# Stick-breaking attention in a two-block kernel: GpSimd sums the softplus of later key blocks, and one projection tile is cut in two between the two heads' products

## The chip, the cores and the metric

The kernel runs on one core of a Trainium2 chip. The metric is device time in microseconds of one execution, from the first to the last instruction of the program. Five engines work at the same time and wait for each other through semaphores: PE (TensorE, matrix products into the PSUM banks), DVE (VectorE, elementwise), ACT (ScalarE, activations and copies), POOL (GpSimd, elementwise, on-chip memory alone) and SP (SyncE, which issues the weight loads). All instructions of an engine run in the order in which the program lists them. A wait of one instruction therefore holds everything behind it on that engine.

## The reference, cut to what matters

The program is a whole network of two blocks. The change is in the second block's stick-breaking attention (8 heads of 64, 512 positions, key blocks of 128):

```
z = jnp.einsum('bqhd,bkhd->bhqk', qb, kb).astype(jnp.float32) * scale
causal = kpos < qpos
log_beta = jax.nn.log_sigmoid(z)
log_1mb = jnp.where(causal, jax.nn.log_sigmoid(-z), 0.0)
later = lax.cumsum(log_1mb, axis=3, reverse=True) - log_1mb
w = jnp.where(causal, jnp.exp(log_beta + later), 0.0)
outs.append(jnp.einsum('bhqk,bkhd->bqhd', w.astype(v.dtype), vb))
```

A weight thus needs the sum of softplus(z) = -log_sigmoid(-z) over all later keys up to the query. Beside this attention the second block projects its input with w_in (26 tiles of 128 columns), and those products are independent of the attention's elementwise work.

## The kernel before, in words

All products are made in a reduced 32-bit format: each operand is split into a high half (a rounded copy, made by ACT) and a low half (the rest, made by DVE as original minus high), and a product is three matmuls: high by high, high by low, low by high. The weights come in slabs of two tiles; `split(n)` on ACT makes the high half of slab n, `split(n)` on DVE the low half (one instruction of 128x2048, 2.3 us), after which `lo_done` counts up and PE may use the slab.

Scores are kept transposed: key block j on the partitions, queries j*128 to 511 along the row. So row j of `softplus` has 128 columns for j = 3 and 512 for j = 0; columns to the left of j*128 in a row are unused. The heads go in four pairs (`first` and `second`), each with its own set of buffers (`softplus` and `softplus_b`). For a pair the order is:

- PE `logits(pair)`: the scores of both heads, j from 3 to 0. The last block (j = 0) waits for the previous pair's output to be read out of its bank (`so_scaled`).
- PE then has two projection tiles, `W_BEFORE[pair]`, as cover. Meanwhile DVE takes the absolute value (`size`), ACT the exponential and logarithm, and DVE adds the positive part and masks the diagonal block with `before` (`softplus_sum`: per row one instruction with an input in PSUM, then one of 128x128 with two inputs in on-chip memory, `sp_ready`). ACT makes `sp_hi`, DVE `sp_lo`, four rows per head each.
- PE `sticks(h)`, for each j: a mask product with `not_before`; the negated sums of the later key blocks, by products with `minus` (all entries -1), high and low for each later block i; and the own block with `from_here`, high and low. ACT `weights(h)` then exponentiates.
- PE makes the projection tile `W_AFTER[pair]` after both heads' sticks, and then `stick_values(pair)`, the products with the values.

DVE's own order in a pair sets much of this: `softplus_sum` of both heads, copy of the first cover tile out of its bank (`w_out_of`), `softplus_low(first)`, copy of the second cover tile, `softplus_low(second)`, and only then `split` of a slab (n+8 in pair 0, n+10 in pair 1, n+11 in pair 2, and a further one, n+9 and n+12, in pairs 0 and 2). Tile 16, made at the end of pair 0, is of slab n+8; tile 19 (pair 1) of slab n+9; tile 22 (pair 2) of slab n+11; tile 25 (pair 3) of slab n+12, where n is the first slab of w_in.

GpSimd makes the masks earlier, and then only issues two small copies of `wk_T` by DMA.

Of the kernel before, what the change touches and what calls it, by code (L numbers as in the profile page):

```python
# [164 lines left out]
def build(nc, ins, out):  # L165
# [9 lines left out]
    with ctx:  # L175
# [209 lines left out]
        v1_stored = sem("v1_stored")  # L385
        v1_loaded = sem("v1_loaded")
# [15 lines left out]
        mixg_ready = sem("mixg_ready")  # L402
        mixg_done = sem("mixg_done")
# [11 lines left out]
        fsum_ready = sem("fsum_ready")  # L415
        stat2_done = sem("stat2_done")
        f_step = sem("f_step")
        v_ready = sem("v_ready")
        y_ready = sem("y_ready")
        col_sqrt = sem("col_sqrt")  # L420
        col_ready = sem("col_ready")
# [8 lines left out]
        pwhi_done = sem("pwhi_done")  # L430
        pwlo_done = sem("pwlo_done")
# [10 lines left out]
        ln_sqrt = sem("ln_sqrt")  # L442
# [56 lines left out]
        sp_low = sem("sp_low")  # L499
        c_ready = sem("c_ready")  # L500
# [65 lines left out]
        def stick_out(h):  # L566
            r0 = (h % 2) * HD
            return bank[3 * (h % 2)][r0:r0 + HD, :]

# [215 lines left out]
        def _(sp):  # L785
# [32 lines left out]
            for n in LOADS:  # L818
# [10 lines left out]
                if n == FIRST["pc_out"] + 2:  # L829
                    sp.wait_ge(kv_free, 32)  # L830
                    sp.dma_start(v1_dram, v1[:, :, :]).then_inc(v1_stored, 16)
                if n == FIRST["mla_o"] + 2:
                    sp.wait_ge(v1_stored, 16)
                    sp.wait_ge(lo_ready, MH // 2)
                    sp.wait_ge(q_ready, MH)
                    sp.dma_start(vN[:, :, :], v1_dram).then_inc(v1_loaded, 16)
# [13 lines left out]
        def _(pool):  # L850
# [70 lines left out]
            pool.wait_ge(tile_free, TILE0["w_in"] + 2 * W_SLABS.index(10) + 1)  # L921
            pool.dma_start(wk_T[HD:, 0, :], wk_T[0:HD, 0, :]).then_inc(k_shift, 16)
            pool.dma_start(wk_T[0:HD, 1, :], wk_T[HD:, 1, :]).then_inc(k_shift, 16)

        @block.tensor
        def _(pe):
# [76 lines left out]
            nc.tensor.transpose(bank[0][:, 0:16], prow[0:16, 0, :], ident[0:16, 0:16]).then_inc(mixg_ready, 1)  # L1003
# [112 lines left out]
            pe.wait_ge(pwlo_done, 1)  # L1116
# [336 lines left out]
            def w_tile(i):  # L1453
# [5 lines left out]
                if i == WV_TILE + 2:  # L1459
# [15 lines left out]
                else:  # L1475
                    slab_tile("w_in", n, i, o[:, :], DT,
                              lambda k: (wh[:, k, j * P:(j + 1) * P], wl[:, k, j * P:(j + 1) * P]), h_operand,
                              free=False)
# [55 lines left out]
            for pair in range(SBH // 2):  # L1534
# [101 lines left out]
            for t in range(NB):  # L1636
# [7 lines left out]
                if t == 0:  # L1644
                    pe.wait_ge(fsum_ready, 1)
# [3 lines left out]
                if t == 2:  # L1649
                    pe.wait_ge(col_sqrt, 1)  # L1650

        @block.scalar
        def _(act):
# [110 lines left out]
            act.wait_ge(mixg_done, 1)  # L1764
# [9 lines left out]
            for s in range(6):  # L1774
# [27 lines left out]
                if s == 3:  # L1802
                    act.wait_ge(small_loaded, 96)
                    a(pw_hi[:, :, :], pw_raw[:, :, :], ACT.Copy).then_inc(pwhi_done, 1)
# [22 lines left out]
            for s in range(8):  # L1827
# [17 lines left out]
                if s == 5:  # L1845
                    act.wait_ge(ln_summed, 2)
                    a(rstd[:, :], stat[:, :], ACT.Sqrt, scale=1.0 / (4 * P), bias=eps[:, :]).then_inc(ln_sqrt, 1)
# [11 lines left out]
            def cross(layer):  # L1859

                for s in range(4):
# [3 lines left out]
                    if s == 1:  # L1865
                        if layer:
                            act.wait_ge(v1_loaded, 16)
# [39 lines left out]
                if layer == 0:  # L1907
                    act.wait_ge(v1_stored, 16)
# [127 lines left out]
            act.wait_ge(v_ready, 1)  # L2036
# [37 lines left out]
            for pair in range(SBH // 2):  # L2074
# [64 lines left out]
            a(kv_col[:, :], bank[7][:, 0:NB], ACT.Sqrt, scale=1.0 / D, bias=eps[:, :]).then_inc(col_sqrt, 1)  # L2139
            act.wait_ge(col_ready, 1)  # L2140
# [6 lines left out]
        def _(dve):  # L2147
# [89 lines left out]
            dve.wait_ge(mixg_ready, 1)  # L2237
            cp(prm[:, 0, 0:16], bank[0][:, 0:16]).then_inc(mixg_done, 1)
# [40 lines left out]
            for s in range(6):  # L2279
# [16 lines left out]
                if s == 5:  # L2296
                    dve.wait_ge(pwhi_done, 1)
                    low(pw_lo[:, :, :], pw_raw[:, :, :], pw_hi[:, :, :]).then_inc(pwlo_done, 1)
# [63 lines left out]
            dve.wait_ge(ln_sqrt, 1)  # L2362
# [378 lines left out]
            stt(v_col, f_weighted, 1.0 / D, t_col, MUL, ADD).then_inc(v_ready, 1)  # L2741
            dve.wait_ge(f_step, 1)
# [13 lines left out]
            dve.wait_ge(f_step, 2)  # L2756
# [167 lines left out]
            def last_square(i):  # L2924
                dve.wait_ge(square_made, DT * len(XNORMS) + i + 1)
                if i > 1:
                    dve.wait_ge(square_added, (DT - 2) * len(XNORMS) + i - 1)
                tt(sq[0][:, :], sq[0][:, :], last_sq[i % 2][:, :], ADD)\
                    .then_inc(square_added if i < DT - 1 else fsum_ready, 1)
# [6 lines left out]
            dve.wait_ge(col_sqrt, 1)  # L2936
            nc.vector.reciprocal(kv_col[:, :], kv_col[:, :]).then_inc(col_ready, 1)
            dve.wait_ge(col_ready, 1)
# [33 lines left out]
```

## Time and profile before

| | us |
|---|---|
| runs shown | 1710.36, 1710.79, 1717.02 |
| median | 1710.79 |
| span of the profiled execution | 1710.9 |
| PE busy in it | 1684.1 |
| DVE busy | 1064.3 |
| ACT busy | 706.7 |
| POOL busy | 23.8 |

The profiled execution's span is within 0.1 us of the median of the runs, so times read from its trace can be added to the median as they are. In the trace every instruction has a start, a duration and, in brackets, the idle time of its engine before it with what ended that time. Durations of matmuls overlap, so what a matmul costs PE is read as the distance between starts. PEclk is the granted clock: 1.00 is the upper level (2.4 GHz), 0.50 the lower (1.2 GHz). The pairs run from 1510 to 1622 us.

### The profile page before, as it was taken

The page shows a single profiled execution, that of the slowest core. Times are in us where ns is not written, and L with a number is a line of the kernel's source. Part 1 is how long each engine was busy: PE and PEld are TensorE (multiplying, and loading weights), DVE is VectorE, ACT ScalarE, POOL GpSimd, SP SyncE. Part 2 cuts the span into 40 slices and gives each one's busy share as a digit, 9 for nine tenths or more (in the row PEclk, how much of TensorE's full clock was granted, in tenths as well). Part 3 has the DMA queues.
Part 4 walks back from the last instruction along what each step waited for, and adds up shares of the span by engine and source line. Part 5 has one row for each costly group of instructions (what it writes and reads, how often), then busy time and mean ns, then how long its engine had stood idle before and what let it go on. Part 6 is the DMA issues. An engine that isn't in the chain of part 4 may idle for free.

```text
span 1710.9 us, 21153 instructions
## 1 busy us (share of the span) xinstructions
PE 1684.1 (98%) x8045; PEld 1374.0 (80%) x8045; DVE 1064.3 (62%) x1513; ACT 706.7 (41%) x1138; POOL 23.8 (1%) x42
## 2 busy tenths in 40 slices
PE   8999999999999999999999999999999999999998
PEld 7888888788888888887668878888888888977776
DVE  5799763475555532478875446555555767357695
ACT  7313543443333322345764264333332113166674
POOL 1000000000000000011100000000000000000000
PEclk9999999999999999999999999999999999999999
DMA  6272522132222232311104203222227641320201
GB/s 208 82 233 79 170 83 68 50 98 90 91 92 95 98 111 93 91 62 42 50 1 148 99 25 98 98 92 92 92 94 243 202 144 57 116 80 25 75 26 49
DMA packets 154295, 164.40 MB, mean 96 GB/s; under 512 B 2999, under 2 KB 150384, under 8 KB 153968
## 3 DMA queue, kind: packets, MB, share of 16 engines
q1 hardware_dynamic: 153408, 162.51, 29.3%
q8 instruction: 48, 0.79, 0.2%
q0 software_dynamic: 336, 0.53, 0.2%
q10 hardware_dynamic: 479, 0.39, 0.1%
q14 instruction: 24, 0.19, 0.0%
HBM read 160.01 MB, written 3.15 MB: 95 GB/s over the span
## 4 chain that ended last, share of the span: by engine, by line
PE 89%; DVE 6%; ACT 3%; issue 1%; DMA 1%; SPq 0%; DVEq 0%; ACTq 0%
PE bank L928 88%; ACT xa_p L1655 1%; DVE w_lo L2159 1%; PE bank L1354 1%; DMA x_nat<-in_x_dram 1%; DVE nmax L2668 0%; DVE h_lo L2159 0%; ACT w_hi L1655 0%; DVE mla_pT_b L2680 0%; ACT mla_p L1655 0%; DVE xa_pT_lo L2159 0%; DVE fb L2748 0%; PE bank L1614 0%; DVE h_lo L2754 0%; DVE mla_q L2629 0%
## 5 line engine op out<-in xcount | busy, mean ns | idle before, releaser
L928 PE MATMUL bank<-h_hi,w_hi 128*128 128x512 f32 x1472 | 578.9, 393 | 3.1 <-DVE w_lo L2159 1.7
L928 PE MATMUL bank<-h_hi,w_lo 128*128 128x512 f32 x1472 | 573.6, 390 | 0.0
L928 PE MATMUL bank<-h_lo,w_hi 128*128 128x512 f32 x1472 | 573.3, 389 | 0.0
L2159 DVE TENSOR_TENSOR w_lo<-w_raw,w_hi 128x2048 fp32r<-128x2048 f32 (+4 forms) x142 | 286.1, 2019 | 232.1 <-ACT w_hi L1655 231.7
L1655 ACT ACTIVATE w_hi<-w_raw 128x2048 fp32r<-128x2048 f32 (+4 forms) x142 | 239.2, 1690 | 393.6 <-PE bank L928 388.1
L928 PEld LDWEIGHTS bank<-h_hi,w_hi 128*128 128x128 f32 x1472 | 276.2, 188 | 67.8 <-issue 7.1
L928 PEld LDWEIGHTS bank<-h_hi,w_lo 128*128 128x128 f32 x1472 | 276.1, 188 | 58.2
L928 PEld LDWEIGHTS bank<-h_lo,w_hi 128*128 128x128 f32 x1472 | 276.3, 188 | 57.9 <-issue 1.2
L928 PE MATMUL bank<-g_hi,w_hi 128*128 128x512 f32 x352 | 137.6, 391 | 0.0
L928 PE MATMUL bank<-g_hi,w_lo 128*128 128x512 f32 x352 | 137.1, 389 | 0.0
L928 PE MATMUL bank<-g_lo,w_hi 128*128 128x512 f32 x352 | 137.0, 389 | 0.0
L1655 ACT ACTIVATE fb<-sq,prm 128x512 f32<-128x512 f32 x44 | 35.9, 817 | 164.9 <-DVE sq L2456 164.9
L2456 DVE TENSOR_TENSOR sq<-bank,rstd 128x512 f32<-128x512 f32 x44 | 30.3, 688 | 94.6 <-PE bank L928 94.6
L2275 DVE SCALAR_TENSOR_TENSOR cv<-glu,prm,cv 128x512 f32<-128x512 f32 x120 | 80.8, 746 | 0.0
L928 PEld LDWEIGHTS bank<-g_hi,w_lo 128*128 128x128 f32 x352 | 66.1, 188 | 13.8
L928 PEld LDWEIGHTS bank<-g_hi,w_hi 128*128 128x128 f32 x352 | 66.1, 188 | 13.6
L928 PEld LDWEIGHTS bank<-g_lo,w_hi 128*128 128x128 f32 x352 | 66.1, 188 | 13.5
L1655 ACT ACTIVATE g_hi<-fb 128x512 f32 (+1 forms) x44 | 27.8, 632 | 105.1 <-DVE fb L2471 105.1
L928 PE MATMUL bank<-m,w_whole 128*128 128x256 f32 x256 | 55.9, 379 | 0.0
L2386 DVE TENSOR_TENSOR x<-x,bank 128x512 f32<-128x512 f32 x32 | 21.9, 685 | 54.5 <-PE bank L928 54.5
L928 PEld LDWEIGHTS bank<-m,w_whole 128*128 128x128 f32 x256 | 48.7, 190 | 6.7
L928 PE MATMUL bank<-mla_k,mla_q 96*128 96x512 f32 (+3 forms) x128 | 42.8, 456 | 0.0
(374 smaller groups left out, 2052.3 us busy)
## 6 DMA issues: line engine op xcount, KB each, us to landing
w_raw<-in_ffn_w_up_dram SPq DMA_DIRECT2D x44, 1024.0 KB, 5.1
w_raw<-in_ffn_w_down_dram SPq DMA_DIRECT2D x16, 1024.0 KB, 5.1
w_raw<-in_w_in_dram SPq DMA_DIRECT2D x13, 1024.0 KB, 5.3
w_whole<-in_xa_wkv_dram SPq DMA_DIRECT2D x12, 1024.0 KB, 5.4
ada_w<-in_w_ada_dram SPq DMA_DIRECT2D x12, 1024.0 KB, 7.8
w_raw<-in_xa_wq_dram SPq DMA_DIRECT2D x8, 1024.0 KB, 5.1
w_raw<-in_xa_wo_dram SPq DMA_DIRECT2D x8, 1024.0 KB, 5.1
w_raw<-in_pc_w_in_dram SPq DMA_DIRECT2D x6, 1024.0 KB, 5.3
```

The lines of the kernel that those rows point to most:

```text
L928: return nc.tensor.matmul(o, w, v, start=start, stop=stop, **kw)
L1354: m = nc.tensor.transpose(o[:, (i - j) * P:(i - j + 1) * P], weights_of(h, i)[:, j * P:(j + 1) * P], ident[:, :])
L1655: return nc.scalar.activation(o, i, f, **kw)
L2159: return tt(lo_, v, hi.bitcast(f32), SUB)
L2275: m = stt(o, src, w, o, MUL, ADD)
L2386: tt(x[:, i, :], x[:, i, :], tile_bank(stage, i)[:, :], ADD).then_inc(tile_free, 1)
L2456: tt(sq[j][:, :], bank[(tile + j) % 4][:, :], rstd[:, :], MUL).then_inc(tile_free, 1)
```

## The change

GpSimd gets four instructions per head that write into the unused left parts of the softplus rows: row 2 gets in columns 0 to 127 a copy of its own block and in 128 to 255 the sum of rows 3 and 2; row 3 gets in columns 0 to 127 a copy of row 1's, and in 128 to 383 the sum of row 1 and row 2's left part. So for j = 1 and j = 0 one product with `minus` per half takes the place of two and three. ACT and DVE now split five pieces per head (128, 512, 384, 384 and 512 columns) instead of four (128, 256, 384 and 512). PE makes the first half (k 0 to 3) of the tile `W_AFTER[pair]` between the two heads' sticks and the second half after them. The two small DMAs of `wk_T` now stand behind the GpSimd instructions of the first two heads. Some semaphores are merged, with the same waits in effect (left out below).

```diff
+        SP_ROWS = ((3, slice(3 * P, T)), (2, slice(0, T)), (1, slice(P, T)), (3, slice(0, 3 * P)), (0, slice(0, T)))
+        SP_NEEDED = {3: 2, 2: 2, 1: 3, 0: 5}
+        BEHIND = {2: (3, slice(3 * P, T)), 1: (2, slice(0, 2 * P)), 0: (3, slice(0, 3 * P))}
...
-            pool.wait_ge(tile_free, TILE0["w_in"] + 2 * W_SLABS.index(10) + 1)
-            pool.dma_start(wk_T[HD:, 0, :], wk_T[0:HD, 0, :]).then_inc(k_shift, 16)
-            pool.dma_start(wk_T[0:HD, 1, :], wk_T[HD:, 1, :]).then_inc(k_shift, 16)
+            for h in range(SBH):
+                one, two, three = (softplus[h % 2][:, i, :] for i in (1, 2, 3))
+                pool.wait_ge(sp_ready, 4 * h + 2)
+                nc.gpsimd.tensor_copy(two[:, 0:P], two[:, 2 * P:3 * P]).then_inc(sum_step, 1)
+                nc.gpsimd.tensor_tensor(two[:, P:2 * P], two[:, 3 * P:], three[:, 3 * P:], ADD).then_inc(sum_ready, 1)
+                pool.wait_ge(sp_ready, 4 * h + 3)
+                nc.gpsimd.tensor_copy(three[:, 0:P], one[:, P:2 * P]).then_inc(sum_step, 1)
+                pool.wait_ge(sum_ready, 2 * h + 1)
+                nc.gpsimd.tensor_tensor(three[:, P:3 * P], one[:, 2 * P:], two[:, 0:2 * P], ADD).then_inc(sum_ready, 1)
+                if h == 1:
...
             def sticks(h):
 
                 for j in range(NB - 1, -1, -1):
-                    pe.wait_ge(sp_low, 4 * h + NB - min(j, 2))
+                    pe.wait_ge(sp_low, 5 * h + SP_NEEDED[j])
                     o = stick(h, j)
                     mm(o[:, 0:P], not_before[:, :], ident_b[:, :], False, False, skip_group_check=True)
-                    for i in range(NB - 1, j, -1):
+                    if j in BEHIND:
+                        i, c = BEHIND[j]
                         for part in (sp_hi, sp_lo):
-                            mm(o[:, (i - j) * P:(NB - j) * P], minus[:, :], part[h % 2][:, i, i * P:], False, False,
-                               skip_group_check=True)
+                            mm(o[:, P:(NB - j) * P], minus[:, :], part[h % 2][:, i, c], False, False, skip_group_check=True)
...
                 sticks(2 * pair)
+                w_tile(W_AFTER[pair][0], 0, DT // 2)
                 sticks(2 * pair + 1)
-                for i in W_AFTER[pair]:
-                    w_tile(i)
+                w_tile(W_AFTER[pair][0], DT // 2, DT)
                 stick_values(pair)
...
-                    for j in range(NB - 1, -1, -1):
-                        act.wait_ge(sp_ready, 4 * h + NB - j)
-                        a(sp_hi[h % 2][:, j, j * P:], softplus[h % 2][:, j, j * P:], ACT.Copy).then_inc(sp_high, 1)
+                    for n_, (i, c) in enumerate(SP_ROWS):
+                        act.wait_ge(sp_ready, 4 * h + (1, 2, 3, 3, 4)[n_])
+                        if n_ in (1, 3):
+                            act.wait_ge(sum_step, 2 * h + (n_ + 1) // 2)
+                            act.wait_ge(sum_ready, 2 * h + (n_ + 1) // 2)
+                        a(sp_hi[h % 2][:, i, c], softplus[h % 2][:, i, c], ACT.Copy).then_inc(sp_high, 1)
...
             def softplus_low(h):
-                for j in range(NB - 1, -1, -1):
-                    dve.wait_ge(sp_high, 4 * h + NB - j)
-                    v = slice(j * P, T)
-                    low(sp_lo[h % 2][:, j, v], softplus[h % 2][:, j, v], sp_hi[h % 2][:, j, v]).then_inc(sp_low, 1)
+                for n_, (i, c) in enumerate(SP_ROWS):
+                    dve.wait_ge(sp_high, 5 * h + n_ + 1)
+                    if n_ < 2:
+                        dve.wait_ge(sum_step, 2 * h + n_ + 1)
+                        dve.wait_ge(sum_ready, 2 * h + n_ + 1)
+                    low(sp_lo[h % 2][:, i, c], softplus[h % 2][:, i, c], sp_hi[h % 2][:, i, c]).then_inc(sp_low, 1)
```

On PE, in pair 0, the end of the first head's sticks before (j = 0: the mask product, three pairs with `minus`, the own block) and the start of the second head's (`_hi_156`, `_lo_154`):

```order
L928 MATMUL bank<-ident_b,not_before 128x128 [waits sp_low]
L928 MATMUL bank<-softplus_hi_155,minus 128x128
L928 MATMUL bank<-softplus_lo_153,minus 128x128
L928 MATMUL bank<-softplus_hi_155,minus 128x256
L928 MATMUL bank<-softplus_lo_153,minus 128x256
L928 MATMUL bank<-softplus_hi_155,minus 128x384
L928 MATMUL bank<-softplus_lo_153,minus 128x384
L928 MATMUL bank<-softplus_hi_155,from_here 128x512
L928 MATMUL bank<-softplus_lo_153,from_here 128x512
L928 MATMUL bank<-ident_b,not_before 128x128 [waits sp_low]
L928 MATMUL bank<-softplus_hi_156,from_here 128x128
```

The same place after the change; `w_hi_55` and `w_lo_57` are the halves of slab n+8 and the row with them the first of tile 16:

```order
L937 MATMUL bank<-ident_b,not_before 128x128 [waits sp_low]
L937 MATMUL bank<-softplus_hi_155,minus 128x384
L937 MATMUL bank<-softplus_lo_153,minus 128x384
L937 MATMUL bank<-softplus_hi_155,from_here 128x512
L937 MATMUL bank<-softplus_lo_153,from_here 128x512
L937 MATMUL bank<-h_hi,w_hi_55 128x512 [waits tile_free,lo_done]
L937 MATMUL bank<-h_lo,w_hi_55 128x512
```

Four of the products with `minus` are gone here (two more for j = 1), and tile 16, with its wait for `lo_done`, has come ahead of the second head's sticks. In pair 2 tile 22 moves in the same way.

On DVE, in pair 0, the low halves of both heads after the change, with the copies of the cover tiles (`sb_gate<-bank`) and the split of slab n+8 (the last row):

```order
L2793 COPY sb_gate<-bank 128x512 [waits slab_half]
L2173 TENSOR_TENSOR softplus_lo_153<-softplus,softplus_hi_155 128x128 [waits sum_ready,sum_step,sp_high]
L2173 TENSOR_TENSOR softplus_lo_153<-softplus,softplus_hi_155 128x512 [waits sum_ready,sum_step,sp_high]
L2173 TENSOR_TENSOR softplus_lo_153<-softplus,softplus_hi_155 128x384 [waits sp_high] x2
L2173 TENSOR_TENSOR softplus_lo_153<-softplus,softplus_hi_155 128x512 [waits sp_high]
L2793 COPY sb_gate<-bank 128x512 [waits slab_half]
L2173 TENSOR_TENSOR softplus_lo_154<-softplus_b,softplus_hi_156 128x128 [waits sum_ready,sum_step,sp_high]
L2173 TENSOR_TENSOR softplus_lo_154<-softplus_b,softplus_hi_156 128x512 [waits sum_ready,sum_step,sp_high]
L2173 TENSOR_TENSOR softplus_lo_154<-softplus_b,softplus_hi_156 128x384 [waits sp_high] x2
L2173 TENSOR_TENSOR softplus_lo_154<-softplus_b,softplus_hi_156 128x512 [waits sp_high]
L2173 TENSOR_TENSOR w_lo_57<-w_raw_53,w_hi_55 128x2048 [waits hi_done]
```

The split has kept its place behind the second head's low halves, which have one more row of 384 columns and one of 512 in place of 256.

On POOL, the first head's four instructions after the change; there were none here before:

```order
L923 COPY softplus<-softplus 128x128 [waits sp_ready]
L924 TENSOR_TENSOR softplus<-softplus 128x128
L926 COPY softplus<-softplus 128x128 [waits sp_ready]
L928 TENSOR_TENSOR softplus<-softplus 128x256 [waits sum_ready]
L923 COPY softplus_b<-softplus_b 128x128 [waits sp_ready]
```

The last row is the second head's first, which waits for that head's second masked row.

## Rows read from the trace of the kernel before

**Rows 1.** The page's busy times of the engines, with their share of the span.
```profile
PE 1684.1 (98%) x8045; PEld 1374.0 (80%) x8045; DVE 1064.3 (62%) x1513; ACT 706.7 (41%) x1138; POOL 23.8 (1%) x42
```

**Rows 2.** Windows of the four pairs, PE alone: length, busy, clock, DMA.
```profile
1512.00:1537.80 25.80, 25.80 (x140) 1.00 0.23 73
...
sum 110.10, PE 109.91; mean PE 27.48
```

**Rows 3.** The chain that ended last, up to the end of pair 0: start, us, what.
```profile
1443.15 94.62 PE bank L928 x536
```

**Rows 4.** Timeline of PE in pair 0: start, duration, instruction.
```profile
1523.35 0.23 PE L928 MATMUL bank<-ident_b,not_before 128*128 128x128 bf16 x1
...
1524.28 0.31 PE L928 MATMUL bank<-softplus_hi,minus 128*128 128x128 f32 x1
...
1524.54 0.33 PE L928 MATMUL bank<-softplus_hi,minus 128*128 128x256 f32 x1
...
1525.21 0.30 PE L928 MATMUL bank<-softplus_hi,minus 128*128 128x128 f32 x1
...
1525.76 0.34 PE L928 MATMUL bank<-softplus_hi,minus 128*128 128x384 f32 x1
...
1529.79 0.40 PE L928 MATMUL bank<-h_hi,w_hi 128*128 128x512 f32 x1
...
1535.35 0.64 PE L928 MATMUL bank<-sb_w,sb_v 128*64 128x512 f32 x1
```

**Rows 5.** Timeline of DVE in pair 0: second masked row, low halves, copy, split.
```profile
1515.59 0.29 DVE L2814 TENSOR_TENSOR softplus<-softplus,before 128x128 f32<-128x128 f32 x1
...
1521.03 1.69 DVE L2159 TENSOR_TENSOR softplus_lo<-softplus,softplus_hi 128x128 fp32r<-128x128 f32 x4
1523.54 0.69 DVE L2779 COPY sb_gate<-bank 128x512 f32<-128x512 f32 x1 [0.82 <-PE bank L928]
1524.15 1.69 DVE L2159 TENSOR_TENSOR softplus_lo<-softplus_b,softplus_hi 128x128 fp32r<-128x128 f32 x4
1525.76 2.29 DVE L2159 TENSOR_TENSOR w_lo<-w_raw,w_hi 128x2048 fp32r<-128x2048 f32 x1
```

**Rows 6.** Timelines of PE and DVE in pair 2.
```profile
1579.82 0.23 PE L928 MATMUL bank<-ident_b,not_before 128*128 128x128 bf16 x1
1580.02 0.69 DVE L2788 COPY sw_gate<-bank 128x512 f32<-128x512 f32 x1 [0.70 <-PE bank L928]
1582.23 2.29 DVE L2159 TENSOR_TENSOR w_lo<-w_raw,w_hi 128x2048 fp32r<-128x2048 f32 x1
```

**Rows 7.** Timeline of ACT in pair 0: behind the high halves; the last exponentials.
```profile
1521.63 1.90 ACT L1655 ACTIVATE w_hi<-w_raw 128x2048 fp32r<-128x2048 f32 x1
...
1531.44 1.45 ACT L1655 ACTIVATE sb_w_b<-bank 128x128 f32<-128x128 f32 x4
```

**Rows 8.** Groups of POOL instructions by shape: busy us, mean ns, idle before.
```profile
L907 POOL TENSOR_TENSOR sq<-sq,rope_sin 128x512 f32<-128x512 f32 x4 | 5.1, 1278 | 88.4 <-DVE sq L2637 88.4
...
L902 POOL TENSOR_TENSOR kpe_raw<-kpe_raw,rope_cos 32x512 f32<-32x512 f32 x1 | 1.6, 1615 | 0.1
...
L857 POOL TENSOR_SCALAR_AFFINE_SELECT ident<-ident 128x128 f32<-128x128 f32 x1 | 0.3, 292 | 0.2 <-POOL iota_i L855 0.2
```

**Rows 9.** Groups of DVE by shape, 700 to 900 us, same columns.
```profile
L2210 DVE SCALAR_TENSOR_TENSOR ckv_lo<-ckv_raw,prm,ckv_hi 128x512 fp32r<-128x512 f32 x2 | 2.9, 1484 | 0.0
...
L2210 DVE SCALAR_TENSOR_TENSOR cq_lo<-cq_raw,prm,cq_hi 128x512 fp32r<-128x512 f32 x3 | 2.1, 745 | 0.0
```

**Rows 10.** Timelines of POOL and DVE where both work.
```profile
802.54 1.37 DVE L2629 SCALAR_TENSOR_TENSOR mla_q<-bank,rstd 64x512 f32<-64x512 f32 x2
...
802.79 1.27 POOL L907 TENSOR_TENSOR sq<-sq,rope_sin 128x512 f32<-128x512 f32 x1 [16.12 <-DVE sq L2637]
```

**Rows 11.** A PE idle time, and windows' busy times and clock behind it.
```profile
806.11 0.22 PE L928 MATMUL bank<-later_b,ident_b 128*128 128x128 bf16 x1 [2.52 <-ACT fb L1655]
...
807.40:810.80 3.40, 3.40 (x13) 2.55 (x12) 3.37 (x9) 2.97 (x7) 0.00 (x0) 0.50 0.00 0
```

More of the change, by code:

```diff
@@ L499, in build @@
         sp_low = sem("sp_low")
+        sum_step = sem("sum_step")
+        sum_ready = sem("sum_ready")
         c_ready = sem("c_ready")
@@ L919, in _ @@
                                     pattern=[[1, P]], channel_multiplier=-1).then_inc(sb_masks, 1)
-            pool.wait_ge(tile_free, TILE0["w_in"] + 2 * W_SLABS.index(10) + 1)
-            pool.dma_start(wk_T[HD:, 0, :], wk_T[0:HD, 0, :]).then_inc(k_shift, 16)
-            pool.dma_start(wk_T[0:HD, 1, :], wk_T[HD:, 1, :]).then_inc(k_shift, 16)
+            for h in range(SBH):
[8 more added lines that the diff above has]
+                if h == 1:
+                    pool.wait_ge(tile_free, TILE0["w_in"] + 2 * W_SLABS.index(10) + 1)
+                    pool.dma_start(wk_T[HD:, 0, :], wk_T[0:HD, 0, :]).then_inc(k_shift, 16)
+                    pool.dma_start(wk_T[0:HD, 1, :], wk_T[HD:, 1, :]).then_inc(k_shift, 16)
         @block.tensor
@@ L1450, in _, with w_tile @@
             ada_columns(ADA // 2 - 1)
-            def w_tile(i):
+            def w_tile(i, k0=0, k1=DT):
                 s, j = i // 2, i % 2
@@ L1458, in w_tile @@
                 wh, wl = view(w_hi[pair_of(n)], DT, 256), view(w_lo[pair_of(n)], DT, 256)
-                if i == WV_TILE + 2:
+                if k0:
+                    pass
+                elif i == WV_TILE + 2:
                     pe.wait_ge(tile_free, TILE0["w_in"] + i)
@@ L1475, in w_tile @@
                 else:
-                    slab_tile("w_in", n, i, o[:, :], DT,
-                              lambda k: (wh[:, k, j * P:(j + 1) * P], wl[:, k, j * P:(j + 1) * P]), h_operand,
-                              free=False)
+                    slab_tile("w_in", n, i, o[:, :], k1 - k0,
+                              lambda k: (wh[:, k0 + k, j * P:(j + 1) * P], wl[:, k0 + k, j * P:(j + 1) * P]), h_operand,
+                              first=k0 == 0, last=k1 == DT, k0=k0, inc=1 if k1 == DT else 0, free=False)
             n = FIRST["w_in"]
@@ L1644, in _ @@
                 if t == 0:
-                    pe.wait_ge(fsum_ready, 1)
+                    pe.wait_ge(f_sums, 3)
                     for b in range(NB):
@@ L1649, in _ @@
                 if t == 2:
-                    pe.wait_ge(col_sqrt, 1)
+                    pe.wait_ge(col_step, 1)
         @block.scalar
@@ L1803, in _ @@
                     act.wait_ge(small_loaded, 96)
-                    a(pw_hi[:, :, :], pw_raw[:, :, :], ACT.Copy).then_inc(pwhi_done, 1)
+                    a(pw_hi[:, :, :], pw_raw[:, :, :], ACT.Copy).then_inc(pw_split, 1)
                 if s == 4:
@@ L1846, in _ @@
                     act.wait_ge(ln_summed, 2)
-                    a(rstd[:, :], stat[:, :], ACT.Sqrt, scale=1.0 / (4 * P), bias=eps[:, :]).then_inc(ln_sqrt, 1)
+                    a(rstd[:, :], stat[:, :], ACT.Sqrt, scale=1.0 / (4 * P), bias=eps[:, :]).then_inc(ln_summed, 1)
                 if s == 6:
@@ L2033, in _ @@
             cross(1)
-            act.wait_ge(v_ready, 1)
+            act.wait_ge(f_step, 1)
             a(r_col, v_col, ACT.Sqrt).then_inc(f_step, 1)
@@ L2138, in _ @@
             act.wait_ge(stat2_done, 4)
-            a(kv_col[:, :], bank[7][:, 0:NB], ACT.Sqrt, scale=1.0 / D, bias=eps[:, :]).then_inc(col_sqrt, 1)
-            act.wait_ge(col_ready, 1)
+            a(kv_col[:, :], bank[7][:, 0:NB], ACT.Sqrt, scale=1.0 / D, bias=eps[:, :]).then_inc(col_step, 1)
+            act.wait_ge(col_step, 2)
             for t in range(NB):
@@ L2235, in pre_copy @@
                     cp(memn[:, r - 4 - DT, :], b[:, 0:MEM]).then_inc(pre_done, 1)
-            dve.wait_ge(mixg_ready, 1)
-            cp(prm[:, 0, 0:16], bank[0][:, 0:16]).then_inc(mixg_done, 1)
+            dve.wait_ge(mixg_step, 1)
+            cp(prm[:, 0, 0:16], bank[0][:, 0:16]).then_inc(mixg_step, 1)
             dve.wait_ge(first_hi, 1)
@@ L2296, in _ @@
                 if s == 5:
-                    dve.wait_ge(pwhi_done, 1)
-                    low(pw_lo[:, :, :], pw_raw[:, :, :], pw_hi[:, :, :]).then_inc(pwlo_done, 1)
+                    dve.wait_ge(pw_split, 1)
+                    low(pw_lo[:, :, :], pw_raw[:, :, :], pw_hi[:, :, :]).then_inc(pw_split, 1)
                 for j in range(2):
@@ L2935, in _ @@
             last_square(DT - 1)
-            dve.wait_ge(col_sqrt, 1)
-            nc.vector.reciprocal(kv_col[:, :], kv_col[:, :]).then_inc(col_ready, 1)
-            dve.wait_ge(col_ready, 1)
+            dve.wait_ge(col_step, 1)
+            nc.vector.reciprocal(kv_col[:, :], kv_col[:, :]).then_inc(col_step, 1)
+            dve.wait_ge(col_step, 2)
             for t in range(NB):
```

41 lines of the change are left out of this document (17 added, 24 removed).

## The prediction

> **What bounds the kernel now.** I read the page's busy times first: PE works 98% of the span, DVE 62%, ACT 41%, POOL 1% [rows 1]. Such a share is an average, so next come windows over the four pairs of heads: PE is busy 109.91 of 110.10 us there, at the upper clock throughout [rows 2]. The chain that ended last agrees: up to the end of pair 0 it runs 94.62 us through PE without a break [rows 3]. So in this stage time is what PE has to do. A product taken from PE is worth its whole slot, and every new wait of PE costs its whole length. Last come the timelines of PE, DVE and ACT in the pairs, for how early each input of PE is ready [rows 4 to 7].
>
> **What PE is spared.** In one head the two products with `minus` for j = 1 that fall away take from 1524.28 to 1524.54, 0.26 us; the four for j = 0 take from 1525.21 to 1525.76, 0.55 us [rows 4]. That is 0.81 us per head and 6.5 us for eight. The sticks of both heads take from 1523.35 to 1529.79, so 3.22 us each; after the change 2.41 us.
>
> **What DVE and ACT get on top.** A head's low halves cover 1280 columns now and 1920 afterwards. Four instructions take 1.61 us until the next one begins (1524.15 to 1525.76) [rows 5]; in proportion 2.42 us, 0.8 us more per head. ACT's high halves grow by about as much, 1.6 us a pair. They were finished at 1521.63 [rows 7]; at 1523.2 they are still ahead of the second head's low halves, which begin at 1524.15 [rows 5]. That costs nothing; without this cover it would be those 1.6 us.
>
> **The tile that is cut in two.** This decides the sign. Tile 16 in pair 0 and tile 22 in pair 2 come from a slab whose low half DVE makes only behind the second head's low halves of that same pair, as the order of DVE shows. Before, PE asked for that slab at 1529.79 and DVE had it at 1525.76 + 2.29 = 1528.05 [rows 4, 5]: 1.7 us to spare. Now PE asks after the first head's sticks, at 1523.35 + 2.41 = 1525.76. DVE is later than before: its first 0.8 us go into the 0.82 us that it idled before copying the second cover tile, the second 0.8 us do not, and the slab is ready at 1528.85. PE waits 3.1 us. In pair 2 PE asks at 1579.82 + 2.41 = 1582.23, DVE's idle time is 0.70 us, and the slab is ready at 1582.23 + 2.29 + 0.8 + 0.1 = 1585.42: 3.2 us [rows 6]. Queued behind the waiting tile on PE are the second head's sticks, the tile's second half and the values; the whole pair shifts. Tiles 19 and 25 are of slabs that were split a pair earlier, so pairs 1 and 3 have no such wait. Sum so far: -6.5 + 6.3 = -0.2 us.
>
> After the second head's sticks only half a tile is left to cover ACT's exponentials: (1535.35 - 1529.79)/2 = 2.78 us against 1.45 us [rows 4, 7]. This costs nothing; without the cover it would be 1.45 us a pair.
>
> **GpSimd's four instructions.** None of these shapes with this operation is in the trace. An add of 128x512 took 1.28 us [rows 8], so in proportion 0.32 us for 128 columns and 0.64 for 256; a copy I take from the 128x128 mask, 0.29 us. A head's chain is then some 1.6 us from its second masked row, and ACT asks for the sums later than that, so the chain alone is hidden. The upper bound is 1.6 us each whatever the width, as for the 32x512 product [rows 8]; that is a rival below.
>
> What is not hidden is the two engines together. Beside GpSimd's products at 752 to 757 us, two VectorE instructions with two inputs in on-chip memory took 1484 ns in the mean, where the same form took 745 ns elsewhere [rows 9]. With one input in PSUM they kept their 0.68 us each beside GpSimd's product at 802.79 [rows 10]. In `softplus_sum` the masking multiplies have two on-chip inputs, and DVE has no idle time between them and the split. The third row's multiply falls into GpSimd's 128-column add, and the fourth's into the 256-column add. I take 0.7 us per head: about 0.25 and 0.45 us, the parts of 0.32 and 0.64 us that are left when the multiply arrives. The bounds are nothing (GpSimd yields) and 1.6 us per add.
>
> The Trainium skill (SBUF — State Buffer, section "SBUF: two separate sides") speaks against this change: GpSimd and a VectorE instruction with two SBUF inputs exclude each other for a whole instruction, and the loser blocks fully. By it the wait could be the whole 0.32 + 0.64 us per head, and the sum below 1.2 us higher; the 1484 ns agree in kind, and are 0.74 us per instruction, less than one whole 1.6 us product.
>
> With 0.7 us per head the slab comes 1.4 us later in pairs 0 and 2: PE waits 4.5 and 4.6 us, 9.1 in all. In pair 0 the first head's low halves start at 1522.4 in place of 1521.03, and their first two pieces (a third of 2.42 us) are ready at 1523.2, when PE wants them at 1523.35 [rows 4, 5]: at the edge. For pairs 1 and 3 I put 0.2 us of wait each. Sum: -6.5 + 9.1 + 0.4 = +3.0 us.
>
> **The clock.** PE idled 2.52 us until 806.11, and from 807.40 to 810.80 the granted clock was 0.50, the lower level [rows 11]. The new waits are longer than that one. A stretch of 3.4 us at half speed loses at most 1.7 us; part of it will fall into the wait itself, so I take 0.85 us for each of the two waits, with 0 and 1.7 as bounds. Sum: +3.0 + 1.7 = +4.7 us, on a median of 1710.8: **1715.5 us**.
>
> The two DMAs of `wk_T` still wait for the copy of tile 16. Behind them on POOL now stand the sums of pairs 1 to 3, which nobody asks for before the next pair's logits. The merged semaphores add no instruction.
>
> **The rivals.**
> - *GpSimd and VectorE hardly touch.* Then only the two waits of 3.1 and 3.2 us stand: -0.2 us, plus 0 to 1.7 us of clock: 1710.6 to 1712.3, say 1711.4. For it: VectorE's instructions with an input in PSUM were not slowed [rows 10]. Against it: those with two on-chip inputs were [rows 9].
> - *GpSimd becomes the bound* (slower). If each of its four instructions takes 1.6 us [rows 8], both heads need 12.8 us from the first head's second masked row at 1515.9 [rows 5], until 1528.7. After that come one high half (an estimate of 0.5 us), the last two low pieces (896 of 1920 columns, 1.1 us) and the split (2.29 us): 1532.6, where the sum above has 1528.05 + 2.2 = 1530.25. So pairs 0 and 2 are 2.4 us longer: 4.7 + 4.8 = +9.5 us, 1720.3. It decides once the two heads' eight instructions need more than about 10.4 us, for then the second head's low halves wait for them. For it: the trace has no such short add. Against it: 0.29 us for a 128x128 instruction.
> - *The change does what it says and nothing waits:* -6.5 us, 1704.3. It needs the slabs of tiles 16 and 22 ready some 3 us earlier than DVE's order allows. Against it: both orders and [rows 5, 6].
>
> **How the numbers follow.** Chances: the forecast 0.60, GpSimd and VectorE apart 0.24, GpSimd the bound 0.11, nothing waits 0.05. The forecast's own range reaches from 1713.8, with no fall of the clock (+3.0), to 1718.4, with two full falls (another 1.7) and whole adds waited for (another 1.2). The range of 1709.5 to 1719.0 takes in the forecast and the first rival and leaves out the other two, 0.16. A measurement of this kernel tells some 0.5%, or 8.5 us, from no change: below 1702.3 no case reaches, 0.02 for what I have missed; above 1719.3 lies most of the second rival, 0.10; the rest, 0.88, is no change.
>
> **What the profile after would show.** Six fewer products per head and 2.4 us of sticks; in pairs 0 and 2 an idle time of PE of 3 to 4.6 us before the first matmul of tiles 16 and 22, ended by DVE's `w_lo`, and none of that kind in pairs 1 and 3; masking multiplies above 0.29 us where GpSimd adds; a clock of 0.50 for a few us behind the long waits. The forecast is wrong if those two waits are under 2 us, or if PE waits for `softplus_lo` in every pair.

## The result, and the profile after

The changed kernel took 1717.12 us in the median of 20 runs (1714.48 to 1722.69), the kernel before 1710.88 us (20 runs, 1708.59 to 1717.02) on the same chip: a ratio of 1.0036, with a 95% interval of 1.0028 to 1.0044, so 4.8 to 7.5 us slower. That is inside the 0.5% that the prediction calls no change, and 1.6 us above its 1715.5.

The page's busy times say almost nothing about it, and answer to [rows 1]. PE has 48 products fewer and is busy 1.2 us less, in a span that is 5 us longer:

```profile
PE 1682.9 (98%) x7997; PEld 1370.6 (80%) x7997; DVE 1073.1 (63%) x1521; ACT 712.0 (41%) x1146; POOL 37.5 (2%) x74
```

Windows over the four pairs, PE alone, tell where the time went. A window reaches here from a pair's first logits to the next pair's, and the last one to the end of the last pair's values; the columns are length, PE's busy time, granted clock, DMA share and GB/s.

```profile
1509.05:1541.57 32.52, 29.09 (x141) 0.90 0.21 65
1541.58:1568.67 27.09, 27.03 (x146) 1.00 0.17 50
1568.68:1600.71 32.03, 28.41 (x142) 0.95 0.19 66
1600.72:1627.40 26.68, 26.61 (x142) 1.00 0.12 40
sum 118.32, PE 111.14; mean PE 27.79
```

The same four windows of the kernel before:

```profile
1509.96:1537.64 27.68, 27.68 (x153) 1.00 0.20 65
1537.65:1566.08 28.43, 28.37 (x158) 1.00 0.19 57
1566.09:1594.12 28.03, 27.96 (x154) 1.00 0.23 76
1594.13:1622.13 28.00, 27.94 (x154) 1.00 0.11 38
sum 112.14, PE 111.95; mean PE 27.99
```

So pairs 1 and 3 became 1.3 us shorter each and pairs 0 and 2 became 4.8 and 4.0 us longer: +6.2 us, the measured difference. In pairs 0 and 2 PE is now idle for over 3 us, and the clock is not at 1.00 throughout.

The timeline of PE in pair 0 shows both (start, duration, instruction, idle time before it and who ended it); its last two lines are from pair 2. It answers to [rows 4].

```profile
1522.44 0.23 PE L937 MATMUL bank<-ident_b,not_before 128*128 128x128 bf16 x1
...
1523.38 0.36 PE L937 MATMUL bank<-softplus_hi,minus 128*128 128x256 f32 x1
...
1523.70 0.34 PE L937 MATMUL bank<-softplus_hi,from_here 128*128 128x384 f32 x1
...
1524.09 0.42 PE L937 MATMUL bank<-softplus_hi,minus 128*128 128x384 f32 x1
...
1524.52 0.39 PE L937 MATMUL bank<-softplus_hi,from_here 128*128 128x512 f32 x1
...
1528.58 0.80 PE L937 MATMUL bank<-h_hi,w_hi 128*128 128x512 f32 x1 [3.43 <-DVE w_lo L2173]
1529.17 0.63 PE L937 MATMUL bank<-h_lo,w_hi 128*128 128x512 f32 x1
...
1533.87 0.27 PE L937 MATMUL bank<-ident_b,not_before 128*128 128x128 bf16 x1
...
1536.43 0.40 PE L937 MATMUL bank<-h_hi,w_hi 128*128 128x512 f32 x1
...
1588.65 0.79 PE L937 MATMUL bank<-h_hi,w_hi 128*128 128x512 f32 x1 [3.55 <-DVE w_lo L2173]
...
1593.04 0.23 PE L937 MATMUL bank<-ident_b,not_before 128*128 128x128 bf16 x1
```

The first half of tile 16 waits 3.43 us for the low half of its slab, and then its 12 matmuls last 0.62 to 0.80 us each and 5.29 us together (1528.58 to 1533.87), where the second half at 1536.43 has the usual 0.39 to 0.40 us a matmul. The first half of tile 22 in pair 2 waits 3.55 us and takes 4.39 us (1588.65 to 1593.04). The reason for the slow halves is in windows of the two stretches of low clock, whose columns are the length, the busy times of PE, PEld, DVE, ACT and POOL, then the clock, DMA share and GB/s:

```profile
1527.10:1533.93 6.83, 5.35 (x13) 3.88 (x14) 3.40 (x2) 4.79 (x7) 0.00 (x0) 0.50 0.51 154
1588.54:1591.95 3.41, 3.30 (x8) 2.62 (x9) 2.26 (x2) 0.00 (x0) 0.00 (x0) 0.50 0.66 191
```

The first stretch begins 1.48 us before its wait ends, the second 0.11 us before.

The list of PE's waits from 1500 to 1640 us names no other of that kind (total, times, longest), so pairs 1 and 3 have none:

```profile
PE bank L937 <- DVE w_lo L2173: 7.0, 2, 3.6
```

The chain that ended last ran through PE alone up to the end of pair 0 before [rows 3]. Now it leaves PE at 1511.53, runs through VectorE's list and comes back when the slab is split (start, length, what):

```profile
1520.36 0.68 DVE sb_gate L2793
1521.04 1.80 DVE softplus_lo L2173 x5
...
1523.30 0.68 DVE sb_gate L2793
1523.98 2.34 DVE softplus_lo L2173 x5
1526.32 2.21 DVE w_lo L2173
...
1528.58 13.12 PE bank L937 x58
```

In the timeline of VectorE in pair 0, which answers to [rows 5], the third and fourth masking multiplies of a head take 0.43 and 0.57 us in place of 0.29, and five low halves take 2.34 us until the next instruction (the copy at 1523.30 in the chain above) where four took 1.61:

```profile
1515.48 0.43 DVE L2828 TENSOR_TENSOR softplus<-softplus,before 128x128 f32<-128x128 f32 x1
...
1516.55 0.57 DVE L2828 TENSOR_TENSOR softplus<-softplus,before 128x128 f32<-128x128 f32 x1
...
1520.96 2.42 DVE L2173 TENSOR_TENSOR softplus_lo<-softplus,softplus_hi 128x128 fp32r<-128x128 f32 x5
```

GpSimd's timeline beside it has the two adds of this head, of 128 and of 256 columns, which none of the rows before could price:

```profile
1515.30 0.47 POOL L924 TENSOR_TENSOR softplus<-softplus 128x128 f32<-128x128 f32 x1
...
1516.23 0.74 POOL L928 TENSOR_TENSOR softplus<-softplus 128x256 f32<-128x256 f32 x1
```

### The profile page after: what moved, and what is told of

Its sections match the earlier page's. It is cut to its first block, busy times and chain, and to the rows that moved or that the text cites. A ratio compares the mean times of both kernels' runs of the same rounds, so it can differ in the third digit from the quotient of the medians.

```text
span 1715.9 us, 21137 instructions
## 1 busy us (share of the span) xinstructions
PE 1682.9 (98%) x7997; PEld 1370.6 (80%) x7997; DVE 1073.1 (63%) x1521; ACT 712.0 (41%) x1146; POOL 37.5 (2%) x74
## 4 chain that ended last, share of the span: by engine, by line
PE 87%; DVE 7%; ACT 3%; issue 1%; DMA 1%; SPq 0%; POOL 0%; DVEq 0%; ACTq 0%
PE bank L937 86%; ACT xa_p L1666 1%; DVE w_lo L2173 1%; PE bank L1363 1%; DMA x_nat<-in_x_dram 1%; DVE softplus_lo L2173 1%; DVE nmax L2682 0%; DVE h_lo L2173 0%; ACT w_hi L1666 0%; DVE mla_pT_b L2694 0%; ACT mla_p L1666 0%; DVE xa_pT_lo L2173 0%; DVE fb L2762 0%; PE bank L1625 0%; DVE h_lo L2768 0%
```

## The experiments

**The theory, T.** The products spared bring some 5.3 us, twice what pairs 1 and 3 gained. What is lost is 7.3 us of waiting, because the halved tile asks for its slab before VectorE has split it, in pairs 0 and 2, and 4.2 us of low clock behind those waits. **R1:** GpSimd's work beside VectorE is itself the cost. **R2:** the longer high and low halves make TensorE late wherever the tile stands.

The table has all runs. "Pairs" is the length of the four windows together, from the first logits to the last values, as the profile's windows sum it; the last column is the ratio of each kernel to the kernel before, measured on the same chip.

| kernel | pairs, us | to before | median, us | ratio (95% interval) |
|---|---|---|---|---|
| before | 112.14 | | 1711 to 1712 | |
| changed | 118.32 | +6.2 | 1717.12 | 1.0036 (1.0028 to 1.0044) |
| e1_whole | 109.27 | -2.9 | 1708.19 | 0.9980 (0.9971 to 0.9989) |
| e2_halved | 115.55 | +3.4 | 1714.92 | 1.0015 (1.0005 to 1.0025) |
| e3_pool | 112.11 | 0.0 | 1711.36 | 0.9999 (0.9988 to 1.0010) |
| e4_products | 106.68 | -5.5 | 1705.43 | 0.9960 (0.9948 to 0.9973) |
| e5_warm | 114.34 | +2.2 | 1713.19 | 1.0005 (0.9997 to 1.0014) |
| e6_split_first | 109.67 | -2.5 | 1708.53 | 0.9982 (0.9973 to 0.9991) |
| e7_high_first | 108.47 | -3.7 | 1706.95 | 0.9974 (0.9963 to 0.9986) |
| e8_pool_mask | 107.70 | -4.4 | 1706.98 | 0.9970 (0.9958 to 0.9981) |
| e9_mask_high_first | 107.00 | -5.1 | 1707.55 | 0.9976 (0.9965 to 0.9986) |

The intervals are 2.7 to 4.3 us wide; the windows tell kernels apart that the medians can't.

**e1_whole: the tile whole again.** Everything else of the change stays.

```diff
                 sticks(2 * pair)
-                w_tile(W_AFTER[pair][0], 0, DT // 2)
                 sticks(2 * pair + 1)
-                w_tile(W_AFTER[pair][0], DT // 2, DT)
+                w_tile(W_AFTER[pair][0])
```

> The changed kernel with the projection tile whole again, behind both heads' products. Theory T (the products spared bring 5.3 us, and what is lost again is the wait of tiles 16 and 22 for the late low half of their slab, 3.6 us each, with the clock that falls behind it): behind both heads' products the tile asks about 2.5 us later, so waits of about 1.0 us are left in pairs 0 and 2, none in pairs 1 and 3, and no fall of the clock. 5.3 - 2.0 is 3.3 us faster than the kernel before, about 1707.6 us. Rival R1 (GpSimd beside VectorE is itself the cost): its instructions are all still there, so the kernel stays slower than before, by 3 us or more. Rival R2 (the longer high and low halves make TensorE late wherever the tile stands): slower than before too, with a wait ahead of the second head's products.

It is 1.9 to 5.0 us faster than the kernel before: the change without its halving is a gain, so both rivals fall. PE's waits in the stage (the two slabs):

```profile
PE bank L937 <- DVE w_lo L2172: 1.9, 2, 1.0
```

The four windows are at clock 1.00, as T had it. The 1.0 us of wait that is left has two sources: there were 1.7 us to spare, VectorE has the slab 1.4 us later in the pair than before, and PE, with fewer products, asks 1.3 us earlier.

**e2_halved: the halving alone,** put into the kernel before, with all 80 products by `minus` and no sums. The part left out lets `w_tile` make half a tile, as in the change.

```diff
...
                 sticks(2 * pair)
+                w_tile(W_AFTER[pair][0], 0, DT // 2)
                 sticks(2 * pair + 1)
-                for i in W_AFTER[pair]:
-                    w_tile(i)
+                w_tile(W_AFTER[pair][0], DT // 2, DT)
```

> The kernel before with the projection tile split between the two heads' products and nothing else: no sums on GpSimd, all 80 products. T: the first half of tiles 16 and 22 asks for its slab some 3.2 us earlier than the whole tile did, so it waits about 1.5 us in pairs 0 and 2 (VectorE has less to do ahead of the slab than in the changed kernel), none in pairs 1 and 3; 3 us slower with the clock kept, up to 6 if it falls behind the waits: 1714 to 1717 us. R1 and R2: the sums are not there and so is no loss, within 1 us of the kernel before.

0.9 to 4.3 us slower, 3.4 in the windows, so halving costs without any of GpSimd's work; R1 and R2 expected less than 1 us. The waits are 2.7 of these 3.4 us (first line, from the list of waits), and the first half of tile 16 begins behind 1.37 us (second line, from the timeline):

```profile
PE bank L928 <- DVE w_lo L2161: 2.7, 2, 1.4
...
1525.93 0.50 PE L928 MATMUL bank<-h_hi,w_hi 128*128 128x512 f32 x1 [1.37 <-DVE w_lo L2161]
```

The four windows are again at 1.00: after waits of this length the clock stayed up, with those of 3.4 and 3.6 us it fell.

**e3_pool: GpSimd's four instructions alone,** put into the kernel before. No product reads the sums, and the low halves wait until GpSimd is done with the rows.

```diff
+            for h in range(SBH):
+                ...
+                pool.wait_ge(sp_ready, 4 * h + 2)
+                nc.gpsimd.tensor_copy(two[:, 0:P], two[:, 2 * P:3 * P]).then_inc(sum_ready, 1)
+                nc.gpsimd.tensor_tensor(two[:, P:2 * P], two[:, 3 * P:], three[:, 3 * P:], ADD).then_inc(sum_ready, 1)
+                ...
             def softplus_low(h):
+                dve.wait_ge(sum_ready, 4 * h + 4)
```

> The kernel before with GpSimd's four instructions of each head added and nothing else: no product reads the sums, and VectorE's low halves wait until GpSimd is done with the rows. T: VectorE's masking multiplies take 0.1 us longer each, 0.4 us for each head, and the whole tile stands far enough behind that TensorE is not late: less than 1 us slower. R1: several us slower (4 or more), as the changed kernel is.

No difference, in the windows (112.11 against 112.14) or in the time. The masking multiplies do get longer, by more than in the changed kernel (426 and 423 ns in the mean for the two buffers, where they took 292 before):

```profile
L2825 DVE TENSOR_TENSOR softplus<-softplus,before 128x128 f32<-128x128 f32 x16 | 6.8, 426 | 0.5
L2825 DVE TENSOR_TENSOR softplus_b<-softplus_b,before 128x128 f32<-128x128 f32 x16 | 6.8, 423 | 0.6
```

That is 0.53 us per head, and the whole tile's 1.7 us to spare swallows both heads' share. R1 is out as a cost of its own.

**e4_products: the products spared, and nothing else.** It leaves out the sums of the key blocks beyond the next one.

```diff
-                    for i in range(NB - 1, j, -1):
+                    for i in range(min(NB - 1, j + 1), j, -1):
                         for part in (sp_hi, sp_lo):
```

> The kernel before without the 48 products by minus that the change spares (it leaves out the softplus of every key block beyond the next one), nothing added, tile whole. T: the products alone are worth what the trace of the changed kernel shows, 1.33 us for each pair of heads: 5.3 us faster, about 1706 us, with TensorE as little late as in the kernel before. The forecast's size for this term was 6.5. R1 and R2 say nothing against it. Rival R3 (the spared products run behind other work and bring nothing): the same as the kernel before.

The windows are 5.46 us shorter, 1.37 for each pair; the time 4.6 to 8.9 us. R3 is out: in this stage a product is worth its slot. The windows are precise enough to say that the forecast's 6.5 was too much; the interval of the time holds both.

**e5_warm: TensorE kept busy in the two waits.**

```diff
                 sticks(2 * pair)
+                if pair % 2 == 0:
+                    pe.wait_ge(tile_free, TILE0["w_in"] + W_AFTER[pair][0] - 1)
+                    keep_warm(w_bank(W_AFTER[pair][0]), 16, 4 * P, ident_b[:, :], not_before[:, :])
                 w_tile(W_AFTER[pair][0], 0, DT // 2)
```

> The changed kernel with 16 matmuls of 128x512 in bfloat16, results not used, in the waits ahead of tiles 16 and 22. T: the waits stay as long (the slab is no earlier), the clock stays at full speed behind them, and the first halves take 2.8 us each instead of 5.3 and 4.4: 4.1 us faster than the changed kernel, 2 us slower than the kernel before, about 1713. Rival R4 (the first halves are slow for another reason than the clock, such as the high half of the slab or an operand that comes late): no gain, 1717.

The timeline of PE in pair 0 shows the 16 matmuls in the wait, and the first half behind them at 0.39 to 0.40 us a matmul:

```profile
1525.55 3.63 PE L937 MATMUL bank<-not_before,ident_b 128*128 128x512 bf16 x16
1529.13 0.50 PE L937 MATMUL bank<-h_hi,w_hi 128*128 128x512 f32 x1
1529.47 0.40 PE L937 MATMUL bank<-h_lo,w_hi 128*128 128x512 f32 x1
...
1531.99 0.23 PE L937 MATMUL bank<-ident_b,not_before 128*128 128x128 bf16 x1
```

The half takes 2.86 us in place of 5.29, and the clock is 1.00 in all four windows, while the slab is no earlier: the tile begins 3.58 us after PE is through with the first head. These sum to 114.34, 3.98 us less than in the changed kernel: that is the clock's whole share, and R4 is out.

**e6_split_first: VectorE's order.** The low half of the slab goes ahead of the second head's low halves in pairs 0 and 2; the tile stays halved.

```diff
-                softplus_low(second)
+                if pair % 2:
+                    softplus_low(second)
                 if pair < 2:
                     split(n + 8 + 2 * pair)
                 else:
                     split(n + 7 + 2 * pair)
+                if pair % 2 == 0:
+                    softplus_low(second)
```

> The changed kernel, tile halved, with VectorE's low half of the slab moved ahead of the second head's low halves in pairs 0 and 2. T: the slab is there 2.3 us earlier, so the wait ahead of tiles 16 and 22 falls from 3.6 us to about 1.2, the clock falls not at all or for one stretch, and the second head's low halves still come before the first half of the tile is done: about 2.8 us faster than the kernel before, 1708 us. R1: the same as the changed kernel, since GpSimd's work is unchanged, 1717. R2: the second head's low halves come 2.3 us later and TensorE waits for them instead, 1716 to 1718.

The same instructions in another order give 8.65 us of the stage back, 118.32 to 109.67, with the clock at 1.00. VectorE's timeline, and below it PE's list of waits:

```profile
1520.89 2.29 DVE L2173 TENSOR_TENSOR w_lo<-w_raw,w_hi 128x2048 fp32r<-128x2048 f32 x1
1523.10 2.42 DVE L2173 TENSOR_TENSOR softplus_lo<-softplus_b,softplus_hi 128x128 fp32r<-128x128 f32 x5
```

```profile
PE bank L937 <- DVE w_lo L2173: 2.3, 2, 1.2
```

No wait for the second head's low halves is in that list, which R2 expected, and R1 expected no gain.

**e7_high_first: ScalarE's order too.** In pairs 0 and 2 the slab's high half goes ahead of the second head's high halves, and VectorE's copy of the second covering tile behind the slab's low half.

```diff
                         a(sp_hi[h % 2][:, i, c], softplus[h % 2][:, i, c], ACT.Copy).then_inc(sp_high, 1)
-                if pair < 2:
-                    split(n + 8 + 2 * pair)
...
+                    if h % 2 != pair % 2:
+                        continue
+                    if pair < 2:
+                        split(n + 8 + 2 * pair)
...
-                w_out_of(W_BEFORE[pair][1])
-                softplus_low(second)
+                if pair % 2:
+                    w_out_of(W_BEFORE[pair][1])
+                    softplus_low(second)
...
+                if pair % 2 == 0:
+                    w_out_of(W_BEFORE[pair][1])
+                    softplus_low(second)
```

> As the kernel in which VectorE's low half of the slab goes ahead of the second head's low halves, and in pairs 0 and 2 ScalarE's high half of the slab goes ahead of the second head's high halves too, and VectorE's copy of the second covering tile behind the slab. T: the low half can begin 0.6 us earlier, so a wait of 0.6 us is left in place of 1.2: 1 us faster than that kernel, about 4 us faster than the kernel before. Rival: the second head's low halves, which now wait for later high halves, make TensorE late at its second products, and it is no faster than that kernel or slower.

The waits fall to 1.1 us for both slabs, 0.6 at most, and the windows by 1.20 us; the medians of e6 and e7 were measured on different chips, and their intervals overlap.

```profile
PE bank L937 <- DVE w_lo L2175: 1.1, 2, 0.6
```

**e8_pool_mask: GpSimd masks.** The tile is whole, and VectorE's masking multiplies are gone.

```diff
-                    link(stt(v, stick(h, j), 0.0, v, MAX, ADD))
-                    tt(v[:, 0:P], v[:, 0:P], before[:, :], MUL).then_inc(sp_ready, 1)
+                    stt(v, stick(h, j), 0.0, v, MAX, ADD).then_inc(sp_raw, 1)
...
+                def mask(j):
+                    pool.wait_ge(sp_raw, 4 * h + NB - j)
+                    v = softplus[h % 2][:, j, j * P:(j + 1) * P]
+                    nc.gpsimd.affine_select(out=v, in_=v, compare_op=ALU.is_gt, fill=0.0, base=0,
+                                            pattern=[[1, P]], channel_multiplier=-1).then_inc(sp_ready, 1)
...
```

> The changed kernel with the tile whole, and with GpSimd masking the diagonal blocks (affine_select in place) instead of VectorE's multiplies. T: VectorE's list gets 3.3 us shorter in each pair, less what it now waits for GpSimd; the slab is there in time for the whole tile, and no wait of tiles 16 and 22 is left: 5.3 us faster than the kernel before, 2 us faster than the changed kernel with the whole tile. R1 (GpSimd's work beside VectorE costs): slower than the changed kernel with the whole tile, since GpSimd has twice the instructions. Rival R5: GpSimd needs 0.46 us or more for a mask, its list of a head is 3.6 us and longer than VectorE's share was, so the high and low halves start later and TensorE waits for them by 1 us in a pair: no faster than that kernel.

A mask on GpSimd takes 0.29 us, not the 0.46 that R5 feared:

```profile
L927 POOL TENSOR_SCALAR_AFFINE_SELECT softplus<-softplus 128x128 f32<-128x128 f32 x16 | 4.7, 291 | 138.0 <-DVE softplus L2838 137.9
```

The stage is 1.57 us shorter than with the tile whole and the masks on VectorE; T expected 2. VectorE's timeline shows what is left. The first head's low halves take 2.92 us instead of 2.42, beside GpSimd's work for the second head, but that is not it: behind them VectorE idles 0.54 us, until PE is done with the second covering tile. From there the copy, the second head's low halves and the split take 5.2 us, and PE's products for both heads 5.1:

```profile
1520.20 2.92 DVE L2184 TENSOR_TENSOR softplus_lo<-softplus,softplus_hi 128x128 fp32r<-128x128 f32 x5
1523.66 0.69 DVE L2804 COPY sb_gate<-bank 128x512 f32<-128x512 f32 x1 [0.54 <-PE bank L949]
1524.27 2.42 DVE L2184 TENSOR_TENSOR softplus_lo<-softplus_b,softplus_hi 128x128 fp32r<-128x128 f32 x5
1526.61 2.28 DVE L2184 TENSOR_TENSOR w_lo<-w_raw,w_hi 128x2048 fp32r<-128x2048 f32 x1
```

So PE is still a little late, where T expected no wait:

```profile
PE bank L949 <- DVE w_lo L2184: 0.5, 2, 0.2
```

R1, which had this kernel slower than e1, is wrong again.

**e9_mask_high_first: e7 with GpSimd's masks.** The edits are those of e7 and e8, with the tile halved.

> The changed kernel, tile halved, with GpSimd masking and with the slab's high and low halves ahead of the second head's in pairs 0 and 2. The slab's low half should be there about 0.7 us before the first half of tiles 16 and 22 asks (in the kernel with GpSimd's masks VectorE is done with the first head's low halves 13.0 us behind the pair's start, and 2.3 us of splitting end at 15.3, while TensorE asks at 16.0), so no wait is left: the four pairs take 106.8 us, 5.4 less than in the kernel before, which is 0.9 less than with the whole tile and GpSimd's masks. About 1706 us. Rival: the second head's low halves come last and are late now, 0.5 us or more ahead of the second head's products in pairs 0 and 2; then the pairs take 108 us or more.

PE's list has no wait for a slab left, and none for low halves. The pairs sum to 107.00, against the 106.8 expected:

```profile
sum 107.00, PE 106.70; mean PE 26.68
```

Its median does not beat those of e7 and e8, though its stage is the shortest of the three: 0.7 to 1.5 us is less than the medians can tell. All three are faster than both kernels. What the cut of the tile is itself worth no run shows, since none moves the slab ahead and leaves the tile whole; e4, whole and without a wait for a slab, has 106.68, so nothing here points to a gain from the cut.

## Why the prediction was right

Sign, size and place of the effect were right, and the two waits stood where the prediction put them. Its terms, in its own order:

- **Products.** The forecast was 0.81 us per head, 6.5 in all; e4 measured 5.46, and the changed kernel's pairs 1 and 3 give 5.3 for all four. The step took the slots of the products that go and left those that stay as they were. But the product that follows the bfloat16 mask product costs more there: before, it was always a 128-column one; now it is the 256- or the 384-column one. The two 256-column products took 0.28 us behind two others (1524.54 to 1524.82 in the kernel before) and 0.32 directly behind the mask (1523.38 to 1523.70); the two of 384 columns 0.34 (1525.76 to 1526.10) and 0.43 (1524.09 to 1524.52). That is 0.13 us per head, 1.0 in all, which is what was missing. Why a wider product costs more in that place no run settles. The kernel before, in the lines behind those of [rows 4]:

```profile
1524.82 0.34 PE L928 MATMUL bank<-softplus_hi,from_here 128*128 128x384 f32 x1
...
1526.10 0.39 PE L928 MATMUL bank<-softplus_hi,from_here 128*128 128x512 f32 x1
```

- **Low halves and high halves.** 0.8 us more per head forecast, 0.73 measured, and ScalarE's longer list was covered, as said: PE waits for `softplus_lo` nowhere, nor for the exponentials behind the half tile. The 0.2 us of wait that were put down for pairs 1 and 3 did not come.
- **The tile cut in two.** The prediction has this step deciding the sign, and e1, e2 and e6 show that it does: take the cut away, or hurry the slab, and the change gains 2.5 to 2.9 us in the stage. The waits were forecast at 4.5 and 4.6 us. In PE's timeline of pair 0 the first head's products and the wait take 6.14 us (1522.44 to 1528.58), the second head's products, which do not wait, 2.56 (1533.87 to 1536.43): 3.6 us of wait, and 3.7 by the same subtraction in pair 2.
- **GpSimd beside VectorE.** 0.7 us per head forecast; 0.14 + 0.28 = 0.42 measured, which for two heads is 0.56 of the 0.9 us by which a wait was shorter than forecast. Another 0.15 us is the first head's products, 2.56 us where 2.41 was forecast, so that PE asked later. The first rival (the two hardly touch) had less still and would have given 1711.4; the rival of GpSimd as the bound needed adds of 1.6 us and they took 0.46 and 0.74. Two figures of this step were wrong as written: the 1.28 us of [rows 8] is a product and no add, and whole adds waited for would have added 1.0 us (0.26 for each of four heads), not 1.2, so the forecast's own range ended at 1718.2.
- **The clock.** This term was the most mis-sized: 0.85 us a wait forecast, with 1.7 as the upper bound, and 2.5 and 1.6 us measured (5.29 and 4.39 us for halves that take 2.75), 4.2 in all. The clock itself is 3.98 of them, by e5; the other 0.2 is the first matmul behind a wait, which is 0.34 us ahead of the next at full clock too, where the others are 0.23. The bound failed in pair 0: it rested on one stretch of 3.4 us [rows 11], but there the clock stayed at its lower level for 6.83 us, 5.35 of them behind the wait's end. In pair 2 the stretch was 3.41 us, nearly all of it behind the wait, and cost nearly the whole bound, not half of it.

So the sum of +4.7 was made of -6.5 + 9.1 + 0.4 + 1.7, and the measured +6.2 of -5.5 + 7.3 + 0.1 + 4.2, to 0.1 us (the 0.1 is the halved tiles' own extra time, by pairs 1 and 3 against those of e4): errors of +1.0, -1.8, -0.3 and +2.5, which offset each other in part. The mechanism was right in each of the larger terms; that the time is only 1.6 us off is in part luck, since the waits were 1.8 us too long in the forecast and the clock 2.5 us too cheap.

## What to carry to other kernels

When a tile is moved ahead of other work, look up when the last engine in line has its operand ready, in that engine's own order, before counting the work that is saved: here the gain of 48 products fewer was lost to a demand that came 4 us earlier. If the cut is worth keeping, move the producer with the consumer (e6, e7), and give part of the producer's list to an idle engine (e9; with the tile whole, e8). A wait of TensorE costs more than its length once the clock falls behind it, so waits are not priced by their sum alone: two of 1.4 us left it at 1.00 here (e2), and two of 3.4 and 3.6 us cost another 4 us.

## What the runs showed of the hardware

- Beside GpSimd's adds, a VectorE multiply with two on-chip inputs ended 0.14 to 0.16 us after the add did, whenever it had begun: 1515.48 + 0.43 against an add that ended at 1515.77, and 1516.55 + 0.57 against 1516.97. In e3 the wider add began later beside the multiply, at 1514.81, and ended at 1515.55; the multiply took 0.69 us, from 1515.01 to 1515.70. Alone it takes 0.29 us. It lost what was left of the add when it began, less 0.14 us.
  The Trainium skill (SBUF — State Buffer, section "SBUF: two separate sides") has the two exclude each other for a whole instruction. The rows agree in kind, and the price was 0.42 us per head, where the prediction's bound by it was the adds' whole lengths, 0.32 + 0.64.
- On GpSimd an add of 128 columns took 0.46 us and one of 256 columns 0.74, not in proportion to the 1.28 us of a product of 512 columns [rows 8]; a copy of 128x128 took 0.29 us.
- The granted clock was 0.50 for 6.83 us in pair 0 and for 3.41 us in pair 2, from late in idle times of 3.43 and 3.55 us on. With 1.37 us and less it stayed at 1.00 (e1, e2, e6), and with the wait filled by matmuls too (e5). What makes the one stretch twice as long as the other stays open.
